# Two more weight buffers for every third expert of a mixture-of-experts loop, on one NeuronCore

## The chip, the cores and the metric

One Trainium2 chip, of which the kernel uses one core: TensorE (PE), VectorE (DVE), ScalarE (ACT), GpSimd (POOL) and SyncE (SP), sixteen DMA engines, on-chip memory of 128 partitions and DRAM outside. The metric is the device time of one launch in microseconds (us), lower is better; the median of several runs counts.

## The reference, cut to what matters

Two layers of a hybrid backbone over 384 tokens (128 context, 256 latent) of width 1024. Each layer has four token mixers, a gated merge, and then a mixture of experts, which is the part that matters here. A token goes to the best of 4 groups and to the best 2 of the 4 experts in it. Each of the 16 experts is a SwiGLU of hidden width 512:

```python
for gi in range(N_GROUPS):
    a = jnp.einsum('bsd,edf->bsef', h, p['w_e1'][gi])
    b = jnp.einsum('bsd,edf->bsef', h, p['w_e3'][gi])
    y = y + jnp.einsum('bsef,efd->bsd', jax.nn.silu(a) * b * w_all[:, :, gi, :, None], p['w_e2'][gi])
```

All is float32: an expert's three matrices are three blocks of 2 MB (w_e1 and w_e3 interleaved as input blocks 0 and 1, w_e2 as output block 2), 96 MB per layer.

## The kernel before

Every engine has a program of its own, written out by hand, and semaphores order them. All weights are streamed from DRAM by SyncE, in blocks of 128 partitions x 4096 floats, into six slots: `ring[0..2]` are buffers of their own, `ring[3..5]` are parts of the tile `pc`, which is free in the expert loop. `weight_uses` gives each block its slot; `have` is TensorE's wait for a block, `fill` SyncE's load of one.

The expert loop runs over e = 0 to 15. Experts 0, 1 and 15 are fixed; the places between are given to the experts in an order sorted by load (`order_of`, computed by VectorE from the router, L2574), so that their weights can only be addressed when that is known. An expert takes up to 64 rows of tokens, a wide place (e = 0, 1, 4, 6, 8, 15) up to 96. The steps of place e:

- GpSimd scatters all token rows into a table in DRAM once before the loop, six indirect DMAs (L2783), when `slot_of` is ready. ScalarE waits until all six have landed (L1805), and then `load_rows(1)` and `load_rows(2)` load rows back (L1793; L1795 for the third part of a wide place). Place 0 needs no such load: its rows are picked by a matmul (L1359). `load_rows(e + 3)` follows after `hidden(e)`.
- `turn_rows(e)` on TensorE (L1309) transposes the rows as soon as they are in; ScalarE copies them to `x_h` (L1774, L1776).
- `hidden(e)` (L1319, and L1324 if wide) multiplies them by input blocks 0 and 1; ScalarE's silu (L1815) and VectorE's product (L2625) make the hidden rows `x_g`, which lie in `ytok[:, 2]`.
- `turn_hidden(e)` (L1350, L1352) transposes them, `project(e, n)` (L1340; L1335 for place 15) multiplies by the output block. VectorE copies the result out (L2616), ScalarE stores it to DRAM (L1801).

TensorE's order is hidden(0), turn_rows(1), turn_hidden(0), hidden(1), turn_rows(2), project(0), turn_hidden(1), hidden(2), and so on, up to hidden(14), turn_rows(15), project(13), turn_hidden(14), project(14), hidden(15). After the loop GpSimd gathers the expert outputs of each token (L2793), and project(15) and a product with the picks (L1425) end the layer.

SyncE's order in the loop: the blocks of places 0 and 1 are loaded ahead of it (three are issued at about 643 us, one at 662, two at 679 in the first layer). Then it waits until `order_of` is ready, and for each e it waits until `hidden(e)` is done and loads the input blocks of place e + 2 into the slots that this frees, and waits until `project(e - 1)` is done and loads the output block of place e + 1. Input blocks alternate between two pairs of slots, output blocks between slots 2 and 5.

GpSimd zeroes the two row tables once in the first layer (L2696), two DMAs of 6 MB from a tile of zeros; it waits for them at L2769. GpSimd's own DMAs need descriptors, for which a scratch is set aside in on-chip memory, by default 16384 bytes of each partition.

## Time and profile before

| | |
|---|---|
| time, 3 runs | median 1884.13 us (1882.58 to 1886.51) |
| the profiled execution | 1894.46 us, span of its instructions 1892.7 us |
| granted TensorE clock, mean | 0.972 of full speed |
| TensorE busy | 1782.1 us (94%) |
| VectorE, ScalarE, GpSimd busy | 813.7, 442.7, 122.4 us |
| moved by DMA | 422.42 MB, of it by SyncE's queue 369.35 MB |
| chain that ended last | TensorE 81%, DMA 14% |
| first expert loop | 704.5 us to about 973 us |
| second expert loop | 1607.8 us to about 1878 us |

All times in the trace count from the span's start. The rows further below are of four kinds. The page has the span cut in 40 slices of 47.3 us. The windows give, for a stretch, the busy time of each engine with the number of its instructions, the granted clock, the mean busy share of the DMA engines and the bandwidth. The timeline gives start, duration, engine, line and operands of instructions, merged where one follows the other; in brackets is the idle time of the engine before, and what ended it. The DMA view gives the packets of each queue in a stretch (q1 is SyncE's queue, q10 ScalarE's, q0 GpSimd's), and for the DMAs issued in it the time from issue to landing.

### The profile page before, as it was taken

To read this page: it belongs to the slowest core of one execution; us is meant where nothing else is said; L and a number is where in the kernel's file an instruction comes from. 1 tells how busy PE (TensorE), PEld (TensorE's weight loads), DVE (VectorE), ACT (ScalarE), POOL (GpSimd) and SP (SyncE) were. 2 spreads that over 40 slices of the span, in tenths; PEclk is the share of its full clock that TensorE was granted. 3 is DMA by queue.
4 is the path that set the end of the run, shared out by engine and by line. 5 is a ranking of instruction groups with operands and counts; after the bars stand their busy time and mean duration, and the time that the engine had idled before them with its cause. 6 is when DMAs were issued, how large, how long until landed. Compare 5 with 4: busy or idle time off the path is not lost.

```text
span 1892.7 us, 25310 instructions
## 1 busy us (share of the span) xinstructions
PE 1782.1 (94%) x10202; PEld 1095.7 (58%) x10202; DVE 813.7 (43%) x1850; ACT 442.7 (23%) x956; POOL 122.4 (6%) x160
## 2 busy tenths in 40 slices
PE   6999999999999989997789999999999998999887
PEld 3445656688777773332245565667888877333223
DVE  1295473565544451111133966536655455111113
ACT  3312344333100121010043134334321112111002
POOL 0001201000000030000020020010000003000002
PEclk9999999999999989998989999999999998999988
DMA  9662293413556658999952221323123335899994
GB/s 403 224 261 91 95 361 106 156 68 112 198 221 270 245 200 353 425 427 426 424 209 101 110 94 58 131 93 120 69 90 112 133 151 201 326 424 425 428 427 156
DMA packets 51926, 422.42 MB, mean 223 GB/s; under 512 B 6448, under 2 KB 7872, under 8 KB 28768
## 3 DMA queue, kind: packets, MB, share of 16 engines
q1 hardware_dynamic: 33696, 369.35, 48.9%
q0 software_dynamic: 9632, 33.07, 5.1%
q10 hardware_dynamic: 8480, 18.35, 2.6%
q8 instruction: 82, 1.34, 0.3%
q14 instruction: 36, 0.29, 0.0%
HBM read 386.38 MB, written 32.28 MB: 221 GB/s over the span
## 4 chain that ended last, share of the span: by engine, by line
PE 81%; DMA 14%; another core or an unknown queue 1%; issue 1%; DVE 1%; ACT 1%; SPq 0%; POOL 0%; ACTq 0%; DVEq 0%
PE psum L871 19%; PE psum L1148 19%; PE psum L1137 9%; PE psum L1319 8%; PE psum L874 7%; DMA pc<-we_in 6%; DMA ring<-we_in 6%; PE psum L1340 2%; PE psum L791 2%; PE psum L1324 2%; DMA ring<-wch_in 2%; PE psum L849 1%; PE psum L1223 1%; PE psum L1335 1%
## 5 line engine op out<-in xcount | busy, mean ns | idle before, releaser
L871 PE MATMUL psum<-hT,ring 128*128 128x384 f32 x1088 | 363.9, 489 | 0.1
L871 PEld LDWEIGHTS psum<-hT,ring 128*128 128x128 f32 x1088 | 202.9, 190 | 141.2 <-issue 12.4
L1137 PE MATMUL psum<-pc,ring 128*128 128x384 f32 x512 | 175.6, 486 | 0.0
L1319 PE MATMUL psum<-ring,scr 128*64 128x512 f32 x512 | 126.9, 653 | 30.9 <-DMA ring<-we_in 27.1
L2625 DVE TENSOR_TENSOR ytok<-pc,psum 128x256 f32<-128x256 f32 (+1 forms) x32 | 15.1, 471 | 323.1 <-ACT pc L1815 323.1
L1148 PE MATMUL psum<-hT,ring 128*128 128x192 f32 x768 | 143.0, 329 | 1.8 <-ACT vals L1514 1.8
L1148 PEld LDWEIGHTS psum<-hT,ring 128*128 128x128 f32 x768 | 126.1, 190 | 18.6 <-issue 9.6
L1319 PE MATMUL psum<-pc,scr 128*64 128x512 f32 x512 | 118.0, 615 | 18.7 <-DMA pc<-we_in 18.7
L2015 DVE SCALAR_TENSOR_TENSOR pc<-pc,par 128x384 f32<-128x384 f32 x240 | 127.2, 605 | 0.0
L874 PE MATMUL psum<-ring,hT 128*128 128x512 f32 x288 | 125.2, 593 | 0.0
L1137 PEld LDWEIGHTS psum<-pc,ring 128*128 128x128 f32 x512 | 94.4, 190 | 51.9
L2616 DVE COPY scr<-psum 64x512 f32<-64x512 f32 (+1 forms) x100 | 58.1, 581 | 112.7 <-PE psum L1340 111.9
L1510 ACT ACTIVATE pc<-psum 128x384 f32<-128x384 f32 x72 | 35.2, 490 | 292.0 <-PE psum L871 291.9
L1319 PEld LDWEIGHTS psum<-ring,scr 128*64 128x64 f32 x512 | 43.5, 149 | 103.6 <-issue 101.2
L874 PEld LDWEIGHTS psum<-ring,hT 128*128 128x128 f32 x288 | 54.3, 190 | 66.8 <-issue 65.9
L1319 PEld LDWEIGHTS psum<-pc,scr 128*64 128x64 f32 x512 | 39.8, 141 | 87.4 <-issue 87.4
L1815 ACT ACTIVATE pc<-psum 128x256 f32<-128x256 f32 (+1 forms) x32 | 13.5, 423 | 322.5 <-PE psum L1319 178.5
L1340 PE MATMUL psum<-ring,mva 128*32 128x256 f32 (+1 forms) x512 | 76.2, 502 | 5.7 <-DMA ring<-we_in 5.7
L1148 PE MATMUL psum<-par 128*128 128x192 f32 x304 | 55.6, 326 | 0.0
L1148 PE MATMUL psum<-t_last,ring 128*128 128x192 f32 x304 | 55.6, 326 | 0.0
L1340 PE MATMUL psum<-pc,mva 128*64 128x512 f32 (+1 forms) x288 | 54.9, 550 | 0.0
L1340 PEld LDWEIGHTS psum<-ring,mva 128*32 128x32 f32 (+1 forms) x512 | 25.1, 126 | 48.5 <-issue 38.3
(421 smaller groups left out, 2383.8 us busy)
## 6 DMA issues: line engine op xcount, KB each, us to landing
ring<-we_in SPq DMA_DIRECT2D x48, 2048.0 KB, 17.8
pc<-we_in SPq DMA_DIRECT2D x48, 2048.0 KB, 20.0
ring<-wch_in SPq DMA_DIRECT2D x18, 2048.0 KB, 8.3
ring<-wgate_in SPq DMA_DIRECT2D x16, 2048.0 KB, 8.4
ring<-wmod_in SPq DMA_DIRECT2D x18, 1024.0 KB, 6.7
pc<-wmod_in SPq DMA_DIRECT2D x24, 768.0 KB, 7.7
ring<-wbr_in SPq DMA_DIRECT2D x16, 1024.0 KB, 4.8
ring<-wtok_in SPq DMA_DIRECT2D x6, 2048.0 KB, 8.9
```

The costliest lines, as they stand in the source:

```text
L791: mm = pe.matmul(bank((6, 5, 4)[g])[32 * j:32 * j + 32, :], cond_pad[:, k, shift:shift + 32], w, start=m == first and half == 0, stop=m == ...
L849: mm = pe.matmul(bank(unit_bank(u))[:, 0:T], wv[:, k, u * P:(u + 1) * P], hT[:, k, :], start=k == 0, stop=k == KD - 1)
L871: mm = pe.matmul(F[:, 0:T], wv[:, k, n * P:(n + 1) * P], hT[:, k, :], start=k == 0, stop=k == KD - 1)
L874: mm = pe.matmul(F, hT[:, k, tok(n)], wv[:, k, :], start=k == 0, stop=k == KD - 1)
L1137: mm = pe.matmul(bank(7)[:, 0:T], wv[:, c, (n % 4) * P:(n % 4 + 1) * P], pc[:, MERGE_SLOT[i], c, :], start=c == 0, stop=c == 3)
L1148: mm = pe.matmul(to, weights[:, k, :], tokens[:, k, :], start=opens and k == 0, stop=k == 3, skip_group_check=True)
L1319: mm = pe.matmul(bank(2)[BIG * h:BIG * h + BIG, :], x_h[:, k, 0:BIG], w[h][:, k, :], start=k == 0, stop=k == KD - 1, skip_group_check=True)
L1324: mm = pe.matmul(bank(3)[SUB * c:SUB * c + SUB, 0:256], x_h[:, k, BIG:CAP], w[c // 2][:, k, part], start=k == 0, stop=k == KD - 1, skip_gr ...
L1340: mm = pe.matmul(bank(5 + n)[size * c:size * c + size, 0:width], x_gT[:, f, lo:lo + size], w2[:, f, c * width:(c + 1) * width], start=f == ...
L1510: o = ac.activation(pc[:, b, n, :], B[:, 0:T], ACT.Copy, scale=G_SCALE if b == GQK and n < 2 else 1.0)
L2015: o = ve.scalar_tensor_tensor(dst, src, taps[:, c, j:j + 1], dst, ALU.mult, ALU.add)
L2616: o = ve.tensor_copy(x_y[e % 2][lo:lo + size, c * width:(c + 1) * width], bank(5 + n)[size * c:size * c + size, 0:width])
```

## The change

- The input blocks of every third place (e % 3 == 2, so 2, 5, 8, 11, 14; `spare`) get rooms of their own outside the six slots. Block 0 goes to 3072 columns of `par` and to one tile that holds `t_last` and `zeros` together (1024 columns); block 1 to a new tile `late_room` of 3072 columns and to the first two thirds of `ytok` (1024 columns). Each block is loaded in two DMAs (`fill_spare`), counted on the semaphore `rest_in`.
- The other places' input blocks take the two pairs of slots in turn (`expert_slot`), so three places' input blocks can be held at once. SyncE loads those of place e + 3 when `hidden(e)` is done, and those of place 2 as soon as `order_of` is ready (e = -1), in the first layer also after the zeroing (which reads `zeros`). Output blocks stay as they are: place e + 1 after `project(e - 1)`. The rule that split place 15's input blocks around the output block of place 14 is gone.
- `hidden` takes its weights as a list of views per k.
- To make room, the scratch for GpSimd's descriptors shrinks from the default to 4096 bytes. The zeroing is cut into twelve DMAs of a sixth each.

```diff
@@ -117,6 +117,16 @@
     return chunks + (1 + (before - 1) * KD if before else 0)
 
 
+def spare(e):
+
+    return e % 3 == 2
+
+
+def expert_slot(e, j):
+
+    return 3 * (e % 2) + 2 if j == 2 else 3 * (e % 3) + j
+
+
 def weight_uses():
 
     uses = [((0, ("mod", m)), 3 + m) for m in range(HEAD - 1)]
@@ -124,7 +134,7 @@
         plan = [(block, n % 2) for n, block in enumerate(BLOCKS)]
         plan += [(("gate", i, j), j) for i in range(4) for j in range(2)]
         plan += [(("out", 0), 0), (("out", 1), 1)]
-        plan += [(("exp", e, j), 3 * (e % 2) + j) for e in range(NE) for j in range(3)]
+        plan += [(("exp", e, j), expert_slot(e, j)) for e in range(NE) for j in range(3) if j == 2 or not spare(e)]
         uses += [((l, key), slot) for key, slot in plan]
     return uses
 
...
@@ -167,6 +177,8 @@
 
 
 CAP, BIG = 96, 64
+ZERO_PIECE = 8
+ZEROED = 2 * (NE * CAP // P * 4 // ZERO_PIECE) * 16
 
 FREE = range(2, NE - 1)
 NF_SORT = len(FREE)
...
@@ -281,8 +293,9 @@
         order_of = ctx.enter_context(nc.sbuf_tensor("order_of", [P, NF_SORT], mybir.dt.int32))
         slot_of = ctx.enter_context(nc.sbuf_tensor("slot_of", [P, 2 * NT], mybir.dt.int32))
         slot_back = ctx.enter_context(nc.sbuf_tensor("slot_back", [P, 2 * NT], mybir.dt.int32))
-        zeros = sb("zeros", [P, 256])
-        t_last = sb("t_last", [P, 4 * TH])
+        last_and_zeros = sb("t_last_and_zeros", [P, 4 * TH + 256])
+        t_last, zeros = last_and_zeros[:, 0:4 * TH], last_and_zeros[:, 4 * TH:]
+        late_room = sb("late_room", [P, 3072])
         g_x = [sb("gate_product", [P, T])[:, :], rstd[:, :]]
         spill = ctx.enter_context(nc.sbuf_tensor("spill", [1, 1], mybir.dt.int32))
 
@@ -388,7 +401,9 @@
 
         work = PAR["w_up"][0]
         t_1, t_2, t_4 = (room.rearrange("p (k t) -> p k t", k=4) for room in
-                         (par[:, work:work + 4 * TH], par[:, work + 4 * TH:work + 8 * TH], t_last[:, :]))
+                         (par[:, work:work + 4 * TH], par[:, work + 4 * TH:work + 8 * TH], t_last))
+        spare_rooms = ((par[:, work:work + 3072], last_and_zeros[:, :]),
+                       (late_room[:, :], ytok[:, 0:2, :].rearrange("p t n -> p (t n)")))
         s_rooms = [room.rearrange("p (k n) -> p k n", k=4) for room in
                    (mod_rows[:, :], scr[:, 2304:2816], par[:, work + 8 * TH:work + 8 * TH + 512])]
         s_one, s_sum, s_part = gaT[:, 0:TH], gaT[:, TH:T], scr[:, 2816:2816 + TH]
@@ -438,7 +453,7 @@
         setup_s = sig("setup_step", 0)
         params_in = sig("params_in", 16)
         early_in = sig("first_weights_in", 16)
-        rest_in = sig("rest_of_constants_in", 0)
+        rest_in = sig("rest_of_constants_and_spare_blocks_in", 0)
         slot_in = [sig(f"slot{i}_in", 0) for i in range(6)]
         mod_in = [sig(f"mod_half{i}_in", 0) for i in range(3)]
         mod_done = sig("mod_half_done", 0)
@@ -620,6 +635,22 @@
                 slot = SLOT[l, key][0]
                 sp.dma_start(ring[slot], block_of(l, key)).then_inc(slot_in[slot].sem, 16)
 
+            def fill_spare(l, e):
+
+                for j, rooms in enumerate(spare_rooms):
+                    src, of = block_of(l, ("exp", e, j)), 0
+                    for room in rooms:
+                        width = room.shape[-1]
+                        sp.dma_start(room, src[:, of:of + width]).then_inc(rest_in.sem, 16)
+                        of += width
+
+            def fill_inputs(l, e):
+                if spare(e):
+                    fill_spare(l, e)
+                else:
+                    fill(l, ("exp", e, 0))
+                    fill(l, ("exp", e, 1))
+
             def fill_half(n):
                 m, half = divmod(n, 2)
                 part = slice(half * HALF, (half + 1) * HALF)
@@ -712,20 +743,19 @@
 
                 sp.wait_ge(slot_ready.sem, slot_ready.at(l, 2))
                 expert.clear()
-                for e in range(NE - 1):
-                    if e + 2 in FREE:
-                        p = e + 2 - FREE.start
-                        expert[e + 2] = sp.value_load(order_of[0:1, p:p + 1], min_val=FREE.start, max_val=FREE.stop - 1)
-                    if e < NE - 2:
-                        sp.wait_ge(xab_done.sem, xab_done.at(l, e + 1))
-                        fill(l, ("exp", e + 2, 0))
-                        if e < NE - 3:
-                            fill(l, ("exp", e + 2, 1))
+                for e in range(-1, NE - 1):
+                    if e + 3 < NE:
+                        p = e + 3 - FREE.start
+                        if e + 3 in FREE:
+                            expert[e + 3] = sp.value_load(order_of[0:1, p:p + 1], min_val=FREE.start, max_val=FREE.stop - 1)
+                        if e >= 0:
+                            sp.wait_ge(xab_done.sem, xab_done.at(l, e + 1))
+                        elif l == 0:
+                            sp.wait_ge(rows_zeroed.sem, ZEROED)
+                        fill_inputs(l, e + 3)
                     if e >= 1:
                         sp.wait_ge(xy_done.sem, xy_done.at(l, parts_to(e)))
                         fill(l, ("exp", e + 1, 2))
-                    if e == NE - 3:
-                        fill(l, ("exp", NE - 1, 1))
                 sp.wait_ge(spill_known.sem, spill_known.at(l, 1))
                 spilled = sp.value_load(spill[0:1, 0:1], min_val=0, max_val=1)
                 with sp.If(spilled > 0):
@@ -1313,15 +1343,20 @@
                     pe.wait_ge(xh_ready.sem, xh_ready.at(l, e + 1))
                     if e >= 1:
                         pe.wait_ge(xg_ready.sem, xg_ready.at(l, e))
-                    w = [have(l, ("exp", e, j)) for j in range(2)]
+                    if spare(e):
+                        pe.wait_ge(rest_in.sem, 16 + 64 * (l * len(range(2, NE, 3)) + e // 3 + 1))
+                        parts = [[r.rearrange("p (k n) -> p k n", n=512) for r in rooms] for rooms in spare_rooms]
+                        w = [[r[:, k, :] for r in rooms for k in range(r.shape[1])] for rooms in parts]
+                    else:
+                        w = [[have(l, ("exp", e, j))[:, k, :] for k in range(KD)] for j in range(2)]
                     for k in range(KD):
                         for h in range(2):
-                            mm = pe.matmul(bank(2)[BIG * h:BIG * h + BIG, :], x_h[:, k, 0:BIG], w[h][:, k, :],
+                            mm = pe.matmul(bank(2)[BIG * h:BIG * h + BIG, :], x_h[:, k, 0:BIG], w[h][k],
                                            start=k == 0, stop=k == KD - 1, skip_group_check=True)
                     for k in range(KD if wide(e) else 0):
                         for c in range(4):
                             part = slice(c % 2 * 256, c % 2 * 256 + 256)
-                            mm = pe.matmul(bank(3)[SUB * c:SUB * c + SUB, 0:256], x_h[:, k, BIG:CAP], w[c // 2][:, k, part],
+                            mm = pe.matmul(bank(3)[SUB * c:SUB * c + SUB, 0:256], x_h[:, k, BIG:CAP], w[c // 2][k][:, part],
                                            start=k == 0, stop=k == KD - 1, skip_group_check=True)
                     mm.then_inc(xab_done.sem, 1)
 
...
@@ -2693,9 +2728,11 @@
 
             def zero_rows():
                 for rows_d in (xs_d, ys_d):
-                    gp.dma_start(rows_d.rearrange("(p s) (a n) -> p (s a) n", p=P, n=256),
-                                 zeros[:, :].rearrange("p (a n) -> p a n", a=1).to_broadcast([P, NE * CAP // P * 4, 256]))\
-                      .then_inc(rows_zeroed.sem, 16)
+                    pieces = rows_d.rearrange("(p s) (a n) -> p (s a) n", p=P, n=256)
+                    for i in range(0, NE * CAP // P * 4, ZERO_PIECE):
+                        gp.dma_start(pieces[:, i:i + ZERO_PIECE],
+                                     zeros.rearrange("p (a n) -> p a n", a=1).to_broadcast([P, ZERO_PIECE, 256]))\
+                          .then_inc(rows_zeroed.sem, 16)
 
             for l in range(DEPTH):
                 gp.wait_ge(rows_ready.sem, rows_ready.at(l, 1))
...
@@ -2931,7 +2968,7 @@
     }
     outputs = {"y": (P, KD, T), "ko": (DEPTH, P, H, P), "vo": (DEPTH, P, W), "co": (DEPTH * 8, P, DV + 1),
                "mo": (DEPTH * 2, H, 1), "so": (DEPTH * 8, 64, P)}
-    nc = bacc.Bacc("TRN2", target_bir_lowering=False, num_devices=1)
+    nc = bacc.Bacc("TRN2", target_bir_lowering=False, num_devices=1, dynamic_dma_scratch_size=4096)
     args = [nc.dram_tensor(f"{n}_in", a.shape, F32, kind="ExternalInput").ap() for n, a in arrays.items()]
     args += [nc.dram_tensor(f"{n}_out", s, F32, kind="ExternalOutput").ap() for n, s in outputs.items()]
     args += [nc.dram_tensor(f"{n}_rows", (NE * CAP, D), F32, kind="Internal").ap() for n in ("expert_in", "expert_out")]
```

## Rows read from the trace of the kernel before

**Rows 1.** The page: bandwidth in the 40 slices of the span.
```profile
GB/s 403 224 261 91 95 361 106 156 68 112 198 221 270 245 200 353 425 427 426 424 209 101 110 94 58 131 93 120 69 90 112 133 151 201 326 424 425 428 427 156
```

**Rows 2.** Windows of the first layer's loop and just before it.
```profile
700.00:705.00 5.00, 3.52 (x25) 3.09 (x25) 2.63 (x13) 0.81 (x1) 3.78 (x5) 0.89 0.92 361
705.00:710.00 5.00, 5.00 (x26) 1.71 (x24) 0.00 (x0) 0.00 (x0) 0.47 (x1) 1.00 0.61 239
710.00:715.00 5.00, 5.00 (x72) 2.26 (x68) 0.00 (x0) 1.28 (x1) 0.00 (x0) 1.00 0.46 131
730.00:940.00 210.00, 184.93 (x1086) 69.99 (x1084) 33.55 (x61) 19.95 (x44) 0.00 (x0) 0.95 1.01 425
```

**Rows 3.** Waits of PE from 700 to 960 us: total, times, longest.
```profile
PE psum L1319 <- DMA ring<-we_in: 17.0, 6, 4.6
PE psum L1319 <- DMA pc<-we_in: 7.6, 5, 2.7
```

**Rows 4.** The chain that ended last: start, us, what; a DMA from issue to landing.
```profile
849.15 24.55 DMA pc<-we_in
...
881.65 23.90 DMA pc<-we_in
...
917.14 21.08 DMA ring<-we_in
```

**Rows 5.** Timeline of SyncE, 715 to 730 us: first issues of the loop.
```profile
715.43 0.91 SPq L621 DMA_DIRECT2D ring<-we_in  x2
728.12 0.88 SPq L621 DMA_DIRECT2D pc<-we_in  x2
```

**Rows 6.** Timeline: `order_of` on VectorE, GpSimd's next store, and the zeroing's landing.
```profile
698.02 0.18 DVE L2574 CAST order_of<-sort_key 128x13 int32<-128x13 f32 x1
...
278.20 1.11 POOL L2762 DMA_DIRECT2D so_out<-scr  x2 [40.73 <-ACT scr L1657]
...
expert_out_rows<-zeros POOLq DMA_DIRECT2D x1, 6144.0 KB, 49.4
```

**Rows 7.** Timeline of PE: turn_rows(1), project(14), hidden(15), and hidden(13) of layer two.
```profile
715.15 0.87 PE L1309 MATMUL psum<-cst,pc 128*128 128x128 f32 x6
...
938.26 3.65 PE L1340 MATMUL psum<-ring,mva 128*64 128x512 f32 x16 [2.33 <-DMA ring<-we_in]
943.75 7.09 PE L1319 MATMUL psum<-pc,scr 128*64 128x512 f32 x32 [1.84 <-DMA pc<-we_in]
...
1811.29 10.04 PE L1319 MATMUL psum<-pc,scr 128*64 128x512 f32 x32 [4.66 <-DMA pc<-we_in]
```

**Rows 8.** DMA view: issues in 912.7 to 913 us, and in 728.0 to 728.3 us.
```profile
pc<-we_in SPq DMA_DIRECT2D x1, 2048.0 KB, 20.5
...
pc<-we_in SPq DMA_DIRECT2D x1, 2048.0 KB, 7.8
```

**Rows 9.** DMA queues: 699 to 709, 264 to 270, 720 to 726, 516 to 522 us.
```profile
q0 software_dynamic: 862, 3.14, 80.0%
...
q1 hardware_dynamic: 216, 1.60, 64.1%
q0 software_dynamic: 216, 0.88, 36.1%
...
q1 hardware_dynamic: 157, 2.31, 90.3%
q10 hardware_dynamic: 134, 0.26, 11.3%
...
q1 hardware_dynamic: 608, 2.29, 100.0%
```

**Rows 10.** Row loads: issue of expert 1's second; landing in 710:710.5, 729.6:730.
```profile
710.12 0.44 ACTq L1795 DMA_DIRECT2D pc<-expert_in_rows  x1
...
pc<-expert_in_rows ACTq DMA_DIRECT2D x1, 128.0 KB, 2.7
...
mva<-expert_in_rows ACTq DMA_DIRECT2D x1, 128.0 KB, 15.3
```

More of the change, by code:

```diff
@@ L1873, in _ @@
               .then_inc(setup_s.sem, 1)
-            ve.memset(zeros[:, :], 0.0)
+            ve.memset(zeros, 0.0)
             ve.memset(room32[:, :], float(CAP - BIG))
@@ L2768, in _ @@
                 if l == 0:
-                    gp.wait_ge(rows_zeroed.sem, 32)
+                    gp.wait_ge(rows_zeroed.sem, ZEROED)
                 for n in range(1, KD - 1):
```

## Prediction

> **What bounds the kernel now.** I read the page's slices first. In two stretches, each some 230 us long, the bandwidth stands at 424 to 428 GB/s for slice after slice [rows 1]; these are the expert loops of the two layers. The windows say the same of the first loop: from 730 to 940 us the DMA share is 1.01 at 425 GB/s [rows 2]. So the loop is bound by weight transfers. The waits say at which place TensorE feels it: ahead of `hidden` (L1319), 17.0 + 7.6 us in the first loop [rows 3]. A wait there is for an expert's input block (I below, two blocks of 2 MB per expert); its output block (W) comes just in time. The chain gives the pace: the block that releases expert 11 lands at 849.15 + 24.55 = 873.70 us, that of expert 13 at 881.65 + 23.90 = 905.55 [rows 4]. Two experts, six blocks and their rows, take 31.85 us, which is 15.9 us per expert and 5.3 us per block.
>
> The change pays only by what it does to the stream of blocks. Two facts decide: how far ahead the stream is when it becomes continuous, and which block TensorE waits for last.
>
> **What the change brings.** Before, nothing can be loaded from the end of the preloads until `hidden(0)` is done: SyncE issues I2 at 715.43 and I3 at 728.12 us [rows 5]. After, I2 goes out as soon as the order is known, which is after 698.02 us [rows 6], so from about 699 us. If TensorE's times were unchanged, I3 would be issued at 715.43, I4 at 728.12, and the stream that is continuous from 730 us on would be two blocks further: the nth block after the preloads lands when the (n-2)th did.
>
> That isn't worth two blocks (10.6 us) at the end, because the order of the stream changes as well. Before it runs I(e+2), W(e+1); after it runs I(e+3), W(e+1), so two more blocks lie ahead of every W. Every I lands three blocks earlier, but every W lands just when it did. TensorE no longer waits ahead of `hidden`, it waits ahead of `project` (L1340). What remains is the tail. Before, I15's second block is the last that matters: W14 lands at 917.14 + 21.08 = 938.22 us [rows 4], `project(14)` starts at 938.26 and takes 3.65 us, and `hidden(15)` starts at 943.75 [rows 7]. After, W14 is one place later in the stream, which is two ahead, so it lands when I15's first block did: issued in the window at 912.8, 20.5 us to landing, 933.3 us [rows 8]. `project(14)` ends at 937.0, and `hidden(15)` starts there, 6.7 us earlier. Everything behind it (silu, last project, gathers, residual) hangs on it or on the store after `project(14)`, and moves with it. In the second layer I take the same; its bounds are 4.9 us (only the wait for W14 shrinks) and 7.5. So the gain is 6.7 us per layer, if nothing is late at the start.
>
> **What it costs at the start.** The 4.19 MB of I2 now fall into the time when GpSimd scatters the token rows to DRAM (L2783) and ScalarE loads expert 1's rows back (L1793, L1795), which it may only do when the last scatter has landed. Before, these have the engines alone: 862 packets, 3.14 MB, between 699 and 709 us at a DMA share of 0.92 and 0.61 [rows 2, 9]; the second row load is issued at 710.12 and lands after 2.7 us [rows 10], and TensorE turns the rows at 715.15, directly after `hidden(0)` [rows 7]. The slack is 2.3 us.
>
 So both end together, after 7.33 MB / 425 GB/s = 17.3 us, at about 716.7 us; the scatter, which is through near 709 now, is some 7.6 us later. The row loads go out at about 717.4. By then I3 is queued too (715.43), 16 packets of 16 KB per engine, against the 16 small packets that expert 1's two loads have on each. They take turns again, so the rows are complete when I3 is: (4.19 + 0.39) MB / 425 GB/s = 10.8 us after 716.7, and 0.8 us to land, 728.3 us. TensorE turns them at 715.15 now: it stands for 13.1 us.
> Bounds. Below: the row load doesn't feel I3 and lands in 2.7 us, at 720.1: 5.0 us. Above: one such load beside a continuous stream took 15.3 us [rows 10], 733.2: 18 us. The counted turns are the nearest row, so I take 13.1.
>
> The Trainium skill has this rule too (DMA: Bandwidth & Descriptors, Queues, rings and completion order): each engine goes round robin between its queues, a whole packet of some 9 to 17 descriptors at a time. By the trace the turn is one packet of a record; by the page a turn would hold a whole row load, which could then pass after one block of I3, near 723 us, and the stall would be 8 us in place of 13. By that the sum below would be +8.6 us in place of +18.8.
>
> After such a stand TensorE's clock falls: `hidden(13)` of the second layer, after 4.66 us of idle time, took 10.04 us in place of the 7.09 of `hidden(15)`'s first part [rows 7], 2.95 us more; not every wait is followed by that, so I add 2.5 us (0 to 3). So `hidden(1)` ends 15.6 us later, and with it the issue of I4, which needs its buffers; I4 alone in an idle machine lands 7.8 us after its issue like I3 before [rows 8]. Between I3's end and I4 the DMA queues are empty for some 15 us. The whole stream behind, which bounds the loop, is 15.6 us late, and none of it comes back, since it has no gap to give up.
>
> **The other edits.** The split blocks move in smaller packets. Blocks cut in 6 KB and 2 KB rows ran at 385 GB/s (608 packets, 2.29 MB in 6 us [rows 9]) against 425, 1 us more for an expert's two blocks; 12 KB and 4 KB are nearer to the whole ones. Four of them per layer lie in the bound stretch: 0 to 4 us, I take 0.5. The two more issues by SyncE per spare expert (0.45 us each) are hidden by a queue that is 15 to 25 us deep. The smaller scratch holds fewer descriptors, so GpSimd may have to stay with the twelve pieces of zeroing until most are through; before, it has been idle for 40.73 us when it issues the next store at 278.20 [rows 6], and of the two DMAs of zeroes the second lands 49.4 us after its issue at 235 [rows 6], so that three quarters of all are through before 278. Cost 0; without that cover some us, off the chain. The scatter and the gather have 128 rows each and fit. The wait of SyncE on the zeroes at 699 us was satisfied 400 us before. `hidden` reads the same number of columns from other rooms: 0.
>
> **Sum.** Per layer +13.1 + 2.5 - 6.7 + 0.5 = +9.4 us; two layers +18.8. The profiled execution's span is 1892.7 us (1894.5 in all), 8 to 10 above the median of 1884.1; the difference is put on the median, 1902.9, and I say 1902. Its own range, from the bounds above (stall 8 to 16), is 1892 to 1910.
>
> **Rivals.**
> Free start, the faster side: the scatter and the row loads are not held up, because the small transfers win against the fill. Then only -6.7 x 2 stays: 1870.7. For it: the DMA share is only 0.46 from 710 to 715 us [rows 2], and the slack of 2.3 us. Against: the 216 to 216 turns. The point from which it decides is a stall of 6.3 us; below it the change gains.
> Half a stall: the scatter goes first (709 us), the row loads then share with the rest of I2, 16 turns of 0.37 us, and land at 718.5. Stall 3.3, per layer -3.4: 1877. The Trainium skill says (DMA: Bandwidth & Descriptors, Latency and other measured facts) that strict order between queues works besides round robin; no row shows it.
> Break-even: a stall of 5 to 7 us, as when only the scatter is held up: 1881 to 1887.
> Worse: row loads take 15.3 us, stall 18: per layer +14.3, 1912.
> The change doesn't do what it says: W in place of I as the last wait caps the gain; that is in all cases.
>
> **Chances.** Forecast 0.62, free start 0.10, half a stall 0.12, break-even 0.08, worse 0.08. A measurement of this kernel tells 0.2% from no change, 3.8 us. Faster 0.22, same 0.08, slower 0.70. Leaving out the free start and part of half a stall, the range is 1878 to 1912.
>
> **What would show it.** In the profile after: row loads of expert 1 issued near 717 us and not 710, landing near 728; a wait of 11 to 15 us ahead of L1309 in each layer; a gap of some 15 us in the bandwidth behind I3; then 425 GB/s to the end; the waits on weights at L1340, nearly none at L1319; `hidden(15)` some 9 us later after the loop's start. Wrong if L1309 waits under 6 us, or if weights still hold L1319.

## The result and the profile after

The changed kernel takes 1928.9 us (median of 4 runs, 1923.9 to 1933.7) against 1883.4 for the kernel before (1882.2 to 1886.5): 1.0239 times as long, with a 95% interval of 1.0209 to 1.0269. Beside the experiments on another chip it gave 1.0198 (1.0167 to 1.0229). The forecast was slower, 1902, at most 1912: the direction was right, the size wrong by 27 us, and the range missed.

A caution on profiled executions: that of the kernel before (span 1892.7) is 13 us longer than that of run x8 below (span 1879.5), whose timed runs can't be told from the kernel before (1883.2 and 1883.6 us). Where TensorE's positions are compared below, x8's profile therefore stands for the kernel before, or both are given; its lines are 2 higher than those of before.

The first place is one that the prediction had costed at nothing. GpSimd's timeline of the changed kernel, 230 to 304 us (start, duration, instruction; in brackets the idle time before it):

```profile
232.94 2.69 POOL L2733 DMA_DIRECT2D expert_in_rows<-t_last_and_zeros  x3
246.70 2.64 POOL L2733 DMA_DIRECT2D expert_in_rows<-t_last_and_zeros  x3 [11.07 <-issue]
264.95 2.65 POOL L2733 DMA_DIRECT2D expert_out_rows<-t_last_and_zeros  x3 [15.61 <-issue]
279.30 2.65 POOL L2733 DMA_DIRECT2D expert_out_rows<-t_last_and_zeros  x3 [11.70 <-issue]
281.93 1.11 POOL L2799 DMA_DIRECT2D so_out<-scr  x2
...
298.50 1.05 POOL L2799 DMA_DIRECT2D so_out<-scr  x2 [15.46 <-ACT scr L1692]
```

The twelve pieces of zeroes go out three at a time, and the last three only at 279.30. The stores of `so_out` [rows 6] are now issued 3.7 us later, and above all behind three fresh pieces of zeroes, 1 MB each, in the same queue. Who waits for them, from the waits of 280 to 305 us:

```profile
POOL so_out L2799 <- ACT scr L1692: 15.5, 1, 15.5
...
ACT scr L1692 <- DMA so_out<-scr: 12.8, 1, 12.8
...
PE psum L1075 <- ACT pc L1683: 11.0, 1, 11.0
```

The store reads `scr`; ScalarE may write `scr` again (L1692) only when it has landed, and TensorE waits for what ScalarE does next. TensorE stands 11 us, in a place where nothing held it before.

The second place is the start of each expert loop, where the prediction looked. First the issues of SyncE, then ScalarE's row loads for place 1, TensorE's turn of them, and the landing times of the two loads (DMA view, 741.0 to 741.6 us: KB, us to landing):

```profile
712.39 0.35 SPq L644 DMA_DIRECT2D par<-we_in  x1
...
726.40 0.88 SPq L636 DMA_DIRECT2D ring<-we_in  x2
759.15 0.87 SPq L636 DMA_DIRECT2D pc<-we_in  x2
```
```profile
741.45 1.25 ACTq L1830 DMA_DIRECT2D pc<-expert_in_rows  x1
```
```profile
744.72 1.54 PE L1339 MATMUL psum<-cst,pc 128*128 128x128 f32 x6 [18.55 <-DMA pc<-expert_in_rows]
```
```profile
pc<-expert_in_rows ACTq DMA_DIRECT2D x1, 256.0 KB, 2.8
pc<-expert_in_rows ACTq DMA_DIRECT2D x1, 128.0 KB, 3.2
```

In x8, for the kernel before, the same turn is at 710.94 with 0.60 us of waiting:

```profile
710.94 0.87 PE L1311 MATMUL psum<-cst,pc 128*128 128x128 f32 x6 [0.60 <-DMA pc<-expert_in_rows]
```

All positions up to here are some 14 us later for the zeroes (the first piece of the scatter is issued at 711.01 here, at 696.92 in x8); 18 to 20 us are new. The windows show what they do to the stream (the last two columns are DMA share and GB/s):

```profile
720.00:745.00 25.00, 6.45 (x80) 2.83 (x75) 0.00 (x0) 0.96 (x1) 0.00 (x0) 0.73 0.96 391
745.00:760.00 15.00, 14.79 (x116) 6.93 (x117) 1.03 (x2) 3.60 (x8) 0.00 (x0) 0.88 0.11 32
770.00:950.00 180.00, 159.54 (x951) 57.07 (x949) 27.31 (x50) 17.47 (x38) 0.00 (x0) 0.95 1.01 424
```

The engines are full while I2 and I3 come, then stand empty for 15 us (32 GB/s), until `hidden(1)` has freed buffers and I4 is issued at 759.15; then 424 GB/s as before [rows 2]. The waits of PE from 690 to 970 us, to be held against [rows 3]:

```profile
PE psum L1339 <- DMA pc<-expert_in_rows: 18.5, 1, 18.5
PE psum L1375 <- DMA ring<-we_in: 14.9, 4, 6.0
PE psum L1375 <- DMA pc<-we_in: 6.7, 3, 2.9
```

The weight waits have gone from `hidden` to `project` (L1375) and cost 21.6 us in place of 24.6. So the change did what it was meant to do with the buffers, but it moved the waits more than it shortened them, and set a new one ahead of them. The end of the loop:

```profile
960.50 3.65 PE L1375 MATMUL psum<-pc,mva 128*64 128x512 f32 x16 [1.16 <-DMA pc<-we_in]
...
965.74 3.65 PE L1375 MATMUL psum<-ring,mva 128*64 128x512 f32 x16 [1.21 <-DVE scr L2651]
969.20 7.07 PE L1354 MATMUL psum<-ring,scr 128*64 128x512 f32 x32
```

### The profile page after: what moved, and what is told of

It is laid out like the page before. It is cut to its first block, busy times and chain, and to the rows that moved or that the text cites. A ratio compares the mean times of both kernels' runs of the same rounds, so it can differ in the third digit from the quotient of the medians.

```text
span 1925.9 us, 25524 instructions
## 1 busy us (share of the span) xinstructions
PE 1773.7 (92%) x10202; PEld 1085.5 (56%) x10202; DVE 813.9 (42%) x1850; ACT 443.4 (23%) x956; POOL 127.9 (7%) x170
## 4 chain that ended last, share of the span: by engine, by line
PE 75%; DMA 17%; issue 3%; DVE 2%; POOL 1%; ACT 1%; SPq 0%; ACTq 0%; DVEq 0%; POOLq 0%
PE psum L1178 18%; PE psum L901 17%; PE psum L1167 8%; DMA pc<-we_in 8%; PE psum L1375 5%; PE psum L904 5%; PE psum L1354 5%; DMA ring<-we_in 3%; DMA expert_in_rows<-vals,slot_of 2%; PE psum L821 2%; PE psum L1359 1%; DMA ring<-wch_in 1%; PE psum L879 1%; PE psum L1253 1%; PE psum L1132 1%
## 5 line engine op out<-in xcount | busy, mean ns | idle before, releaser
L1375 PE MATMUL psum<-ring,mva 128*32 128x256 f32 (+1 forms) x512 | 83.7, 534 | 27.6 <-DMA ring<-we_in 25.2
L1354 PE MATMUL psum<-ring,scr 128*64 128x512 f32 x384 | 85.0, 595 | 1.8 <-ACT scr L1809 1.8
L1375 PE MATMUL psum<-pc,mva 128*64 128x512 f32 (+1 forms) x288 | 61.4, 600 | 17.3 <-DMA pc<-we_in 17.3
L1354 PE MATMUL psum<-pc,scr 128*64 128x512 f32 x320 | 72.7, 608 | 0.0
L1375 PEld LDWEIGHTS psum<-ring,mva 128*32 128x32 f32 (+1 forms) x512 | 27.2, 132 | 76.5 <-issue 43.5
L1354 PEld LDWEIGHTS psum<-ring,scr 128*64 128x64 f32 x384 | 27.6, 137 | 51.6 <-issue 49.5
L1178 PE MATMUL psum<-t_last_and_zeros,ring 128*128 128x192 f32 x304 | 55.6, 326 | 0.0
L1869 ACT ACTIVATE mva<-psum 128x256 f32<-128x256 f32 (+1 forms) x32 | 13.6, 424 | 174.5 <-PE psum L1385 140.1
```

Of the source, the lines that this page charges most:

```text
L1178: mm = pe.matmul(to, weights[:, k, :], tokens[:, k, :], start=opens and k == 0, stop=k == 3, skip_group_check=True)
L1354: mm = pe.matmul(bank(2)[BIG * h:BIG * h + BIG, :], x_h[:, k, 0:BIG], w[h][k], start=k == 0, stop=k == KD - 1, skip_group_check=True)
L1375: mm = pe.matmul(bank(5 + n)[size * c:size * c + size, 0:width], x_gT[:, f, lo:lo + size], w2[:, f, c * width:(c + 1) * width], start=f == ...
```

## The experiments

x1 to x4, x5 to x8 and x9 to x12 ran on one chip each. The kernel before takes 1889.9, 1883.6 and 1890.3 us on these three, so between the groups ratios to it are compared, not times.

**Zeroing: x1, x8, x11.** All three are the kernel before with the twelve pieces; they differ in the scratch alone.

```diff
-nc = bacc.Bacc("TRN2", target_bir_lowering=False, num_devices=1)
+nc = bacc.Bacc("TRN2", target_bir_lowering=False, num_devices=1, dynamic_dma_scratch_size=4096)
```

> The kernel before with the smaller scratch and the zeroing in twelve pieces, nothing else. Theory (the zeroing is held up batch by batch by the descriptor space, GpSimd's state stores queue behind it, ScalarE waits for them): a wait of 12 to 13 us for those stores near 285 us, the zeroes through near 297 us in place of 285, and the expert loops as before, rows of place 1 turned directly behind hidden(0): about 1896.5 us. Rival (the small scratch makes every transfer of GpSimd's slow, the scatter of the loop too): the scatter ends 8 us or more after 709 us relative to its start near 699, a wait at the turning of place 1's rows in both layers, 1910 us or more.

x1: 1903.8 us, 1.008 (1.0048 to 1.0112), 14 us more than before. In its trace TensorE waits 9.7 us near 290, where before has no such wait, and the stretch from the scatter to `hidden(1)` is as in before:

```profile
PE psum L1047 <- ACT pc L1650: 9.7, 1, 9.7
```

Held against x8's profile instruction by instruction, x1's is 0.1 us late from 50 to 275 us and 12.5 us late from 300 to 690 us: all of the cost arises at this one place. The wait is 9.7 us of it; for the rest, the granted clock from 280 to 320 us is 0.87, against 1.00 in x8.

> The kernel before with the twelve pieces of zeroes but its own large scratch: one part of the pair that cost 14 us. Theory (GpSimd's issues wait for room for descriptors in the small scratch, so the stores behind are late): with the large scratch all pieces are issued at once, the stores at 278 go out as in before, time within 3 us of before. Rival (twelve pieces cost it themselves, by their number or by what they do in the queues): the time of the run with scratch and pieces, 14 us over before.

x8 (the default scratch): 1883.2 us, 0.9999 (0.999 to 1.0009). The pieces by themselves cost nothing.

> The kernel before with the twelve pieces and a scratch of 8192 in place of 4096: six pieces should find room at once in place of three. Theory (room is given back only when all pieces of a batch have landed): the second six are issued in one go after the sixth has landed, near 262; the last land near 290 in place of 283, so the so stores land 5 to 8 us later than with the large scratch, and the time is 3 to 8 us over before. Rival (each landing gives room for one more piece): GpSimd is through with its issues before 262, the stores land as in before, time within 2 us of before.

x11 (8192): 0.9996 (0.9978 to 1.0014). GpSimd's issues of zeroes in x1, x11 and x8, in this order:

```profile
232.10 2.70 POOL L2700 DMA_DIRECT2D expert_in_rows<-zeros  x3
245.95 2.64 POOL L2700 DMA_DIRECT2D expert_in_rows<-zeros  x3 [11.15 <-issue]
```
```profile
238.73 0.90 POOL L2700 DMA_DIRECT2D expert_out_rows<-zeros  x1
266.98 4.40 POOL L2700 DMA_DIRECT2D expert_out_rows<-zeros  x5 [27.35 <-issue]
278.04 1.11 POOL L2766 DMA_DIRECT2D so_out<-scr  x2 [6.66 <-ACT scr L1659]
```
```profile
237.30 5.27 POOL L2700 DMA_DIRECT2D expert_out_rows<-zeros  x6
277.18 1.11 POOL L2766 DMA_DIRECT2D so_out<-scr  x2 [34.61 <-ACT scr L1659]
```

Three pieces fit into 4096, seven into 8192. Room comes back for a whole batch: in x1 the third piece lands at 245.57 and three more are issued from 245.95, although the first had landed at 240.42; in x11 the seventh lands at 266.55 and five more go out from 266.98. The expectation for x11 had the rule of the batches right, their size wrong by one piece (seven and five, not six and six), and their cost wrong: the last piece lands at 286.2, the first stores at 285.4 and 288.1, 2 to 3 us later than in before, and the slack of ScalarE takes that. So the cost isn't that GpSimd waits; it is that with 4096 the last three pieces are issued just ahead of the stores (279.30 against 281.93), so that the second of these lands at 297.9 and not at 285.5.

**Zeroes elsewhere: x4, and again x9.** The kernel after, with the zeroing begun behind the `vo` store near 366 us, when no one needs GpSimd's queue.

```diff
-                if l == 0:
-                    zero_rows()
...
                 if l == 0:
+                    zero_rows()
                     gp.wait_ge(rows_zeroed.sem, ZEROED)
```

> The changed kernel, with the twelve zeroing DMAs issued behind the last store of the mixers (near 366 us), where GpSimd is idle for some 290 us. Theory: the wait of 12.8 us for the state stores near 285 us goes and nothing takes its place; the loops keep their stall of 18.5 us: the changed kernel less 13, about 1916 us. Rival (the zeroing costs where it stands because it takes bandwidth or GpSimd's time, wherever it is): 1922 to 1929 us, with a new wait between 366 and 450 us.

> The kernel after with the zeroes begun behind the vo store, as in the earlier run of it, now on one chip with the kernel after. Theory (costs add up; the row loads of place 1 are held up twice, by place 2's blocks and by place 3's): 1.012 to 1.016 of before, row loads issued at 718 to 722 and landed at 731 to 735, wait at the turning 14 to 19 us; some 12 us more than with place 3 held back (ratio 1.0083). Rival (the earlier run's distance to that one was its chip's): ratio 1.008 to 1.010.

x4: 1.0146 (1.011 to 1.0182). x9: 1.0144 (1.0117 to 1.0171), beside x12, the kernel after, with 1.0198 on the same chip: 1919.4 and 1931.1 us, 11.7 apart. The wait near 290 is gone, none has come in its place (TensorE waits 0.9 us between 360 and 460 us in x4, as in before), and the loops keep all of their cost: 27 us by the ratio and 29 by the medians, some 14 per layer, where the prediction said 9.4.

> The kernel after once more, beside the others on one chip. Theory (zeroing 13 to 15 us at 290, and 14 to 16 us per layer in the loops): ratio 1.022 to 1.026 of before, and 15 us above the run with late zeroes. Rival (the costs overlap): less than 10 us above it.

x12 fell between the two: 11.7 us above x9, not 15 and not under 10; its ratio of 1.0198 is below the 1.022 to 1.026 that was expected, which its interval just reaches. By the medians the costs of zeroes and loops add up to within 3 us (x1's 13.9 and x9's 29.1 against 40.8 in x12).

**Place 2's blocks later: x2, x3, x6.** The kernel after, with I2 issued only when `hidden(0)` is done (x2) or when place 1's rows have landed (x3, x6; x6 has late zeroes too). The edit of x3:

```diff
-                        elif l == 0:
-                            sp.wait_ge(rows_zeroed.sem, ZEROED)
+                        else:
+                            sp.wait_ge(rows_in[1].sem, rows_in[1].at(l, rows_loaded(1)))
+                            if l == 0:
+                                sp.wait_ge(rows_zeroed.sem, ZEROED)
```

> The changed kernel, with place 2's input blocks loaded only when hidden(0) is done, ahead of place 3's. The small scratch and the split zeroing stay. Theory (the early load collides with the scatter and the row loads): no wait at the turning of place 1's rows; the zeroing still costs 13 us once; the stream of blocks has no head start, so the loops come out within 2 us of before each: 1895 to 1900 us. Rival (the scatter is slow by itself with the small scratch): the wait of 18 us at the turning stays, 1920 us or more.

> The changed kernel, with place 2's input blocks issued when place 1's row loads have landed (near 713 us) in place of right after the order is known. Theory (collision): no wait at the turning; the stream is continuous from 714 us on, 12 us later than the two-block head start wants, so the loops gain 1 to 3 us each at most; with the 13 us of the zeroing 1891 to 1896 us. Rival (the spare rooms and their split blocks are slow themselves): loops longer than before by several us each, 1905 us or more.

> The kernel after with both costs at once taken away: zeroes behind the vo store (near 366 us), and place 2's blocks issued only when place 1's rows have landed. Theory: the two costs add up, so this is the earlier run with place 2 behind the rows (1903) less some 13 us of zeroing: 1887 to 1893, no gain to speak of, because place 2's blocks then start some 3 us later than in before, and of the three-room lead only the tail is left. Rival (the changed order of the stream is worth 6.7 us per layer as predicted, once nothing is late): 1872 to 1880.

x2: 1.0099 (1.007 to 1.0128). x3: 1.0068 (1.0048 to 1.0087). x6: 1.0023 (1.0012 to 1.0034). In none does TensorE stand ahead of the turning (0.2 us at most). x3 costs what x1 does, the zeroes alone, and x2 some 5 us more; both expectations were missed, x3's loops gain nothing where 1 to 3 us each were expected, and x2's cost 2.6 us each, not under 2. In x6 the zeroes' cost is gone too. But x6 is not faster than before: without the stall the new order isn't worth 6.7 us per layer, it costs 2 to 3 us per layer (4.3 in all by the ratio, 5.5 by the medians). Its last projections and `hidden(15)`:

```profile
935.86 3.65 PE L1377 MATMUL psum<-pc,mva 128*64 128x512 f32 x16 [1.74 <-DMA pc<-we_in]
941.10 3.65 PE L1377 MATMUL psum<-ring,mva 128*64 128x512 f32 x16 [1.22 <-DVE scr L2653]
944.55 7.07 PE L1356 MATMUL psum<-ring,scr 128*64 128x512 f32 x32
```

W14 lands at 926.1 + 14.6 = 940.7 us, behind both blocks of I15; before it was 938.2, ahead of I15's second [rows 4, 7]. Its place in the stream is one later (5.3 us), and the stream is ahead by the little that the machine was idle after 715 in before, not by two blocks, since I2 starts at 712.95 here and at 715.43 there [rows 5].

**The stall in parts: x7, x10.** Both have late zeroes. In x7 I2 is early and I3 waits for place 1's rows; in x10 only the first block of I2 is early too.

```diff
-                        elif l == 0:
+                        if e == 0:
+                            sp.wait_ge(rows_in[1].sem, rows_in[1].at(l, rows_loaded(1)))
+                        if e < 0 and l == 0:
```

> The kernel after with late zeroes, place 2's blocks early as there, but place 3's held until place 1's rows have landed. It parts the stall at the turning (in the run with late zeroes row loads were issued at 721.7 and landed at 734.6, where before has 710.1 and 712.8). Theory (turn by turn sharing, twice): the scatter still shares with place 2's blocks, row loads issued near 719 to 722, but then land in 2 to 4 us, near 724; wait at the turning 7 to 10 us in place of 14, per layer 5 us better than with late zeroes: 1905 to 1912 against 1919. Rival (the loss is in the scatter alone, and the share with place 3 costs nothing): the time of the run with late zeroes, 1919, or more. Rival (holding place 3 back costs the stream as much as it saves): 1917 to 1921 with the short wait.

> As with late zeroes, but only the first of place 2's two input blocks goes out as soon as the order is known; the second waits for place 1's rows, and so does place 3's. It scales the cause: half the bytes in the scatter's way. Theory (turn by turn, so the scatter ends some 4 us later in place of 9): row loads issued near 714, landed near 717, wait at the turning 3 to 6 us; time between that with both behind the rows (ratio 1.0023) and that with both early and place 3 held (1.0083): 1889 to 1895. Rival (any fill ahead of the scatter costs the whole, because it is the order of the queues and not the bytes): 1897 to 1901. Rival (one block finds its place in the gap beside the scatter at no cost, and its head start pays): 1874 to 1882.

x7: 1898.3 us, 1.0083 (1.0066 to 1.01). The expected 1905 to 1912 was reckoned for the chip of x4, where it is a ratio of 1.008 to 1.012: met at its lower edge. x10: 1894.1 us, 1.0011 (0.9995 to 1.0026): not between x6's 1.0023 and x7's, as expected, but not to be told from x6.

In x9, with nothing held back, ScalarE's second row load, its landing, and TensorE's turn:

```profile
720.33 0.52 ACTq L1830 DMA_DIRECT2D pc<-expert_in_rows  x1
```
```profile
pc<-expert_in_rows ACTq DMA_DIRECT2D x1, 128.0 KB, 11.8
```
```profile
732.21 1.54 PE L1339 MATMUL psum<-cst,pc 128*128 128x128 f32 x6 [13.84 <-DMA pc<-expert_in_rows]
```

The same three in x7:

```profile
718.96 0.44 ACTq L1832 DMA_DIRECT2D pc<-expert_in_rows  x1
```
```profile
pc<-expert_in_rows ACTq DMA_DIRECT2D x1, 128.0 KB, 2.7
```
```profile
721.68 1.54 PE L1341 MATMUL psum<-cst,pc 128*128 128x128 f32 x6 [11.74 <-DMA pc<-expert_in_rows]
```

The turn in x10:

```profile
718.24 0.87 PE L1344 MATMUL psum<-cst,pc 128*128 128x128 f32 x6 [0.33 <-DMA pc<-expert_in_rows]
```

Counted from the issue of the first piece of the scatter, which is free of all that lies before, place 1's rows are in after (first layer; "more" is against the three kernels of the first line, 14.9, 14.0 and 14.9 us):

```text
kernel                      I2 before the rows   I3 before the rows   us     more than before
before, x8, x6              no                   no                   14-15
x10                         one block            no                   20.8   6 to 7
x7                          two blocks           no                   25.2   10 to 11
after, x4, x9, x12          two blocks           yes                  33.7, 35.7, 35.6, 35.7   19 to 22
```

So each block in front of the scatter costs 5 to 7 us, and I3 beside (or before) the row loads another 8 to 10 (in the second layer x7 has 26.1 us and the last four 33.6 to 36.4). That is the prediction's mechanism, twice, both parts somewhat larger than it said. In x10 `hidden(0)` covers nearly all of it, 0.33 us of waiting in place of the 3 to 6 expected, in part because `hidden(0)` itself begins 2.8 us late there (last section).

**Place 15 early: x5.** The slots and the order of before, but the two blocks of place 15, which is known without the sorting, go into the two new rooms behind the preloads near 678 us, and the loop's stream has two blocks less.

```diff
                 fill(l, ("exp", 1, 2))
+                if l == 0:
+                    sp.wait_ge(rows_zeroed.sem, ZEROED)
+                fill_spare(l, NE - 1)
```

> The slots of before; only place 15, whose weights are known without the order, has its two input blocks in the two new rooms, loaded right behind the preloads, before the scatter, and taken out of the stream of the loop. Zeroing in pieces, small scratch, but begun only behind the vo store near 366 us, where the run with late zeroes had no wait. Theory (the loop's bound is the stream; a room is worth something only if filled while the DMA engines are idle and no small transfer waits): row loads issued near 710 as in before, no wait at the turning, W14 one block sooner and hidden(15) without its own wait: 5 to 8 us per layer, 1868 to 1880 on a chip where before is 1884 to 1890. Rival (the end of the loop is not set by the stream, or two blocks more in the quiet stretch hold up something there): within 3 us of before. Rival (the whole two blocks come back): 21 us less.

x5: 1881.5 us, 0.9994 (0.9982 to 1.0006): no difference that can be told, the rival's answer. The scatter and the row loads are as in before. The end of the loop:

```profile
922.18 7.09 PE L1354 MATMUL psum<-ring,scr 128*64 128x512 f32 x32 [2.68 <-DMA ring<-we_in]
930.00 3.65 PE L1375 MATMUL psum<-pc,mva 128*64 128x512 f32 x16
935.24 3.65 PE L1375 MATMUL psum<-ring,mva 128*64 128x512 f32 x16 [1.21 <-DVE scr L2651]
```

After the wait for I14 nothing waits for weights any more: TensorE's own work, `hidden(14)`, `project(13)`, `project(14)`, takes 16.5 us to `hidden(15)` at 938.70. I14 lands when it did (208 us after the issue of I2, in x8 207), because all that is saved lies behind it. Counted from the issue of I2, `hidden(15)` starts 4.0 us earlier than in x8; in this profile `hidden(0)` starts 2.9 us later, after a stretch at a granted clock of 0.74 (680 to 700 us; 0.91 in x8), so that 1.1 us are left. The low clock need not come from the early loads: in the profile of the kernel before it is 0.69 in the same stretch. No version here beats the kernel before by more than its measurement is uncertain.

## Why the prediction was wrong, step by step

**What bounds the loop** was right: 424 GB/s from 770 to 950 us, and the weight waits go from `hidden` to `project`.

**The smaller scratch, "Cost 0": wrong, and the largest error.** It cost 14 us by itself (x1). The prediction did see that GpSimd would have to stay with the pieces, and named the cover, its 40.73 idle us before the store [rows 6]. The step that failed is what it made of "three quarters of all are through before 278". They all but were (the ninth of twelve pieces landed at 278.95), but in batches of three: the last quarter was therefore issued at 279, just ahead of the stores, where before all of it had been queued at 235 and had 6 us to go. The stores took 15 us to land in place of 5 to 7, and TensorE stood 11 us. A queue whose depth is cut moves work to later, onto whatever is issued next; I asked whether GpSimd had time, not what its stores would find ahead of them. Nor did I follow the store to its reader: "off the chain" was said without looking who waits for `scr`.

**The scatter shares with I2**: right in kind, 10.4 us in place of 7.6 (x7's row loads are issued 22.1 us after the scatter's first piece, before 11.7). The two queues do move one packet for one, but not from the start. The DMA queues of x7 (packets, MB, share), 700 to 705 and 705 to 710 us:

```profile
q1 hardware_dynamic: 108, 1.33, 91.2%
q0 software_dynamic: 29, 0.11, 5.6%
```
```profile
q1 hardware_dynamic: 216, 1.21, 58.0%
q0 software_dynamic: 221, 0.84, 40.9%
```

For some 5 us the scatter gets 29 packets against 108, and both together move 288 GB/s at a share of 0.97, not 425; then 221 to 216. It is the same in the changed kernel (42 to 108 from 714 to 719 us, at 287 GB/s) and much the same in x9 and x10. The 5 us are about the time in which the first of I2's four DMAs moves, 128 packets of 12 KB; the third, of as large packets, shares evenly. The prediction let some ten packets go ahead of the fill and counted 425 GB/s throughout.

**The row loads share with I3**: right, 11.8 us to landing in x9 (2.7 alone), and 10 us of delay from x7 to x9 in place of the 8.2 that follow from the prediction's numbers. In the profile of the changed kernel I3 was issued at 726.40, before the scatter was through, so that the scatter shared with it and the row loads (741.45) did not; in x12 the order was the other one (I3 at 730.94, row loads at 732.46), and the rows were in 33.7 and 35.7 us after the scatter's first piece. So the order of the two makes 2 us of difference at most; the rest goes with the bytes that are ahead or beside. A turn of nine or more descriptors, as the Trainium skill has it (DMA: Bandwidth & Descriptors, Queues, rings and completion order), would have let the row load past after one block. Its 11.8 us beside I3's two blocks speak against it: I3's blocks land at 726.51 and 731.95, it lands at 732.16. The equal counts alone don't, since longer turns of equal length would give them too. Strict order between queues, which the Trainium skill also names (DMA: Bandwidth & Descriptors, Latency and other measured facts), could have let the small transfers go first: nothing of the kind shows, and in the first 5 us the small ones are those that wait.

**The stand and the clock**: 18.5 and 20.2 us in the two layers in place of 13.1, above even the upper bound of 18. This is the term that the loops' sum had mis-sized. By the prediction the rows are in 30.3 us after the scatter's first piece (728.3 less 697.96); measured are 33.7, which is 3.4 of the 5.4 us. The other 2.0 are `hidden(0)`, which ends 15.2 us after that piece in this profile and not 17.2 as in before, so that TensorE stands from earlier on. (In x9 and x12 the wait is 13.8 and 13.9 us, but there `hidden(0)` itself had waited 4.7 us in place of 0.9 and run 1.6 us longer; the rows came 2 us later still.) The turn itself took 1.54 us in place of 0.87, at a granted clock of 0.50; the first part of `hidden(1)` 7.40 (x9: 7.89) in place of 7.09. From the turn to the issue of I4 it is 14.4 us and in the second layer 15.4, in place of the 13.0 from the turn to I3 in before: 1.5 and 2.5 us, as said (2.5).

**The tail, 6.7 us**: too high. From the turn to `hidden(15)` it is 224.5 us in the changed kernel (744.72 to 969.20) and 228.6 in before (715.15 to 943.75): 4.1 us, and in the second layer 1.5 (4.4 and 0.4 against x8). The clock's 1.5 and 2.5 us of the last paragraph are in that; without them the tail is worth 5.6 and 4.0 us. "`hidden(15)` starts there", at the end of `project(14)`, held. What fell short in the first layer is how soon W14 comes: 206.0 us after the issue of I4, where before it comes 210.1 us after that of I3, 4.1 us gained in place of 4.9 (in the second layer 3.1). Nor is W14 the last wait: W13 is (960.50 above, 1.16 us), then `project(13)`, the wait of 1.2 us for VectorE, and `project(14)` follow before `hidden(15)`, 8.7 us in all, and W14 lands in their course, at 965.17. What failed besides is "6.7 us per layer, if nothing is late at the start": x6, with nothing late, has no lead of two blocks either, because I2 can't start early without being in the rows' way. The gain and the cost hang together, and I had costed them as two.

**The sum**: per layer 9.4 predicted, some 14 measured (x9); zeroes 0 predicted, 12 to 14 measured. That is 19 in all against 41 (x12) to 46. The error is 12 to 14 us of zeroes and 8 to 10 of the loops, where the stand is longer and the tail smaller than in the sum.

**The rivals**: free start and half a stall are refuted by x7 (10.4 us with I3 out of the way). x7 is also the case of the break-even rival, only the scatter held up: TensorE waits 11.7 and 9.7 us there, not 5 to 7, and the time is 1.0083 of before. "Worse" (stall 18, 1912) was right for the loops alone: 1883.4 times x9's 1.0144 is 1910.5. The point from which the change gains, a stall of 6.3 us, leaves the clock's 2.5 us out, as half a stall's 1877 does; by the sum's own terms it is 3.7.

**What would show it**. Held: an empty stretch of 15 us (32 GB/s in 745 to 760) and 424 GB/s behind it, the waits on weights at `project` and none at `hidden`. Held with the zeroes out of the way, more or less: row loads near 717 (718.5 in x7, 719.9 in x9; 727 in the changed kernel, if its 14 us are taken off), rows near 728 (732 in x9), 11 to 15 us of wait (13.8 in x9, 13.9 in x12). Not held: the wait in the changed kernel itself, 18.5 and 20.2 us, and `hidden(15)` some 9 us later: counted from the scatter it is 15 us (258.2 after 711.01, against 242.9 after 696.92 in x8; 12 against the profile of before).

What stays open is the first 5 us of the scatter beside a fill, and the late start of `hidden(0)` below.

## What to carry to other kernels

Buffers buy a head start only if something can be loaded in a quiet time; look first at which small, latency-bound transfers live in that quiet time, and count the bytes that will be ahead of each of them: here each 2 MB block ahead of a 3 MB scatter cost 5 to 7 us, and the stream gave only 2 to 4 back for two of them. When the depth of a queue is cut, don't ask whether the issuing engine has time; ask which transfer will now stand behind the last batch, and who waits for the buffer that it reads. And when a reorder lets one kind of block land earlier, find the last wait of the new order by walking its last five steps: here it was neither the block that had been late before nor the one that I had put in its place.

## What the runs showed of the hardware

- GpSimd's DMAs wait for room in the scratch: of pieces of 1 MB three go at a time with 4096, seven with 8192, twelve without a wait at the default size. Room came back 0.4 us after the last of a batch had landed, not after the first.
- When a fill of 12 KB packets starts beside the scatter, the scatter is almost shut out for some 5 us (x7: 29 packets to 108) and the total falls to 288 GB/s, at a share of 0.97; after that it is 221 to 216 and 410 GB/s. I know no reason from these runs.
- In x4, x9, x10 and x12 ScalarE's copy of the turned rows of place 0 starts 2.8 to 3.8 us after TensorE's last turn (x9: 705.27, the turning ended at 701.45), and `hidden(0)` waits 3.6 to 4.7 us for it; in the changed kernel's own profile and in x7, with the same fill, it starts at once (x7: 698.39 after 698.36). ScalarE isn't what is late: in x9 the semaphore that TensorE raises for it goes up at 705.25, 0.02 us before the copy. So either that signal came late or the turning ended later than the profile, which models the ends of matmuls, has it. An early fill alone isn't the reason either: x1, x2, x3 and x11, without one, have 0.9 to 2.2 us there. Not explained.
